# Hybrid decoder trunk on one core: router and shared gate of the first token tile placed ahead of the second tile's turns

## The reference, cut to what matters

```
x = layer_norm(ALPHA * x + g1 * mixed)
h = x * (1 + sc2) + sh2
scores = sigmoid(h @ w_router)            # 64 experts
# top 4 of 8 groups, then top 8 experts of a token, by scores + bias
ffn = (silu(h @ w_sh_gate) * (h @ w_sh_up)) @ w_sh_down + routed_moe(h, ...)
x = layer_norm(ALPHA * x + g2 * ffn)
```

## Time and profile before

| what | value |
|---|---|
| median of three timed runs | 1310.39 us |
| the three runs | 1309.18 to 1311.11 us |
| span of the profiled execution | 1307.3 us |
| PE busy | 1232.3 us (94%) |
| DVE busy | 492.9 us (38%) |
| ACT busy | 249.9 us (19%) |
| HBM read | 492.60 MB, 378 GB/s over the span |

### The profile page before, as it was taken

How to read it: one execution, slowest core, us unless ns; L and a number is a source line. 1 busy time by engine, 2 the same in 40 slices (tenths; PEclk the granted TensorE clock), 3 DMA queues, 4 the chain that set the end, 5 groups by cost and what they waited for, 6 DMA issues and landing times.

```text
span 1307.3 us, 28115 instructions
## 1 busy us (share of the span) xinstructions
PE 1232.3 (94%) x9342; PEld 771.9 (59%) x9342; DVE 492.9 (38%) x1111; ACT 249.9 (19%) x518; POOL 160.7 (12%) x587
## 2 busy tenths in 40 slices
PE   6999999999799999999988999999979999999995
PEld 3474566666466665566546557666646665566563
DVE  5666843222232222233347445222322322133335
ACT  1222211111111111111223312111111111111113
POOL 1000022111011111111000001111111111011110
PEclk9999999999899999999989999999999999899998
DMA  9999979999999999999867956999999999989992
GB/s 316 392 410 399 405 292 421 420 421 421 421 421 420 421 422 420 391 394 406 345 258 288 361 214 234 421 377 422 421 421 420 421 421 421 421 364 392 394 408 104
DMA packets 83921, 494.87 MB, mean 379 GB/s; under 512 B 11970, under 2 KB 20194, under 8 KB 29058
## 3 DMA queue, kind: packets, MB, share of 16 engines
q1 hardware_dynamic: 83842, 493.71, 92.7%
HBM read 492.60 MB, written 1.08 MB: 378 GB/s over the span
## 4 chain that ended last, share of the span: by engine, by line
PE 88%; DVE 4%; DMA 3%; issue 3%; SPq 2%; ACT 1%; DVEq 0%; ACTq 0%
PE ps L1028 32%; PE ps L1050 16%; PE ps L959 9%; PE ps L1071 8%; PE ps L969 5%; PE ps L688 3%; PE ps L881 3%; PE ps L909 2%; DMA w<-in_w_ada 2%; SPq L502 1%; PE ps L810 1%; PE ps L1000 1%; PE ps L1043 1%; PE ps L975 1%; DMA ring<-in_w_ada 1%
## 5 line engine op out<-in xcount | busy, mean ns | idle before, releaser
L1028 PE MATMUL ps<-ring,w 128*64 128x256 f32 (+1 forms) x3648 | 413.3, 385 | 0.5
L1028 PEld LDWEIGHTS ps<-ring,w 128*64 128x64 f32 (+1 forms) x3648 | 259.0, 127 | 68.6 <-issue 14.2
L1050 PE MATMUL ps<-ring,w 128*64 128x512 f32 (+1 forms) x912 | 207.7, 597 | 0.0
L1028 PE MATMUL ps<-flex,w 128*32 128x256 f32 x736 | 170.3, 391 | 26.5 <-issue 26.4
L1028 PE MATMUL ps<-w 128*32 128x256 f32 x736 | 170.8, 392 | 0.0
L1683 DVE SCALAR_TENSOR_TENSOR w<-ps,w 128x256 f32<-128x256 f32 x57 | 27.6, 484 | 374.1 <-PE ps L1028 374.1
L959 PE MATMUL ps<-hx,scat 128*128 128x512 f32 x472 | 138.3, 417 | 0.7 <-issue 0.7
L1669 DVE CAST scat<-ps 128x512 fp32r<-128x512 f32 x114 | 78.9, 692 | 158.9 <-PE ps L1050 158.9
L1028 PEld LDWEIGHTS ps<-flex,w 128*32 128x32 f32 x736 | 81.3, 113 | 84.7 <-issue 42.4
L1208 ACT ACTIVATE w<-ps 128x512 f32<-128x512 f32 x118 | 70.6, 598 | 290.4 <-PE ps L959 290.4
L1071 PE MATMUL ps<-scat 128*128 128x512 f32 x456 | 119.2, 403 | 0.0
(11 more groups left out here) (260 smaller groups left out, 1262.9 us busy)
## 6 DMA issues: line engine op xcount, KB each, us to landing
ring<-in_w_exp_gate SPq DMA_DIRECT2D x88, 1024.0 KB, 19.2
ring<-in_w_exp_up SPq DMA_DIRECT2D x88, 1024.0 KB, 22.3
ring<-in_w_exp_down SPq DMA_DIRECT2D x88, 1024.0 KB, 22.0
ring<-in_w_ada SPq DMA_DIRECT2D x30, 1024.0 KB, 10.9
w<-in_w_exp_gate SPq DMA_DIRECT2D x20, 1024.0 KB, 17.4
w<-in_w_exp_up SPq DMA_DIRECT2D x20, 1024.0 KB, 19.5
flex<-in_w_exp_gate SPq DMA_DIRECT2D x20, 1024.0 KB, 14.5
flex<-in_w_exp_up SPq DMA_DIRECT2D x20, 1024.0 KB, 16.1
```

Of the source, the lines that this page charges most:

```text
L1028: last = mm(ps[unit * g:unit * g + unit, bank, 0:F], hTb[:, kt, unit * g:unit * g + unit], weights(k)[:, kt, :], start=kt == 0, stop=kt == ...
L1050: last = mm(ps[unit * g:unit * g + unit, bank, :], midT[:, f, unit * g:unit * g + unit], down_w(k)[:, f, half * 512:(half + 1) * 512], sta ...
```

## The change

The fillers ahead of tile 1's turns go. In their place PE computes tile 0's logits and both halves of tile 0's shared gate, which need only what ACT has put out. After the turns, tile 1's logits and gate are computed by themselves, block by block as DVE delivers them, so each gate matmul has 128 moving columns instead of 256, and there are 32 of them instead of 16. The logits of both tiles now lie side by side in bank 1; tile 0's gate lies in bank 1 behind them and tile 1's in bank 3. The wait on esc_ready ahead of the up-projection goes, since bank 2 no longer holds logits. In layer 0 a wait on shsil_ready is added ahead of L945, which writes into bank 1. ACT's Exp reads its scores from one bank, and its Silu is two instructions, one for each tile.

```diff
--- before.py
+++ after.py
@@ -359,6 +359,7 @@
         JOB_BANK = (2, 3, 4, 5, 7)
         B_F, B_T, B_0, B_1 = 4, 5, 6, 7
         P0_COL = 448
+        GATE_BANK, GATE_COL = (1, 3), (NT * E, 0)
 
 
         names = """consts_in x_in c_in pos_in eps_set cT_done c32_ready bias_in mod_val_ready acc0_zeroed acc0_bias_in mod1_summed
@@ -901,28 +902,39 @@
                     for g in range(4):
                         last = mm(ps[32 * g:32 * g + 32, 0, :], ones[:, 0:32], acc0[:, g * 512:(g + 1) * 512], start=True, stop=True)
                     last.then_inc(s["p0_summed"], 1)
-                keep_busy(1, 6 if l == 0 else 4)
-                turn_normed(1)
-
                 def shared(w, bank, f, kts=range(KT)):
                     for kt in kts:
                         last = mm(ps[:, bank, f * T:(f + 1) * T], w[:, kt, f * P:(f + 1) * P], xT3[:, kt, :],
                                   start=kt == 0, stop=kt == KT - 1)
                     return last
 
+                def logits(j, kt):
+                    return mm(ps[:, 1, j * E:(j + 1) * E], xT3[:, kt, j * P:(j + 1) * P], router3[:, kt, :],
+                              start=kt == 0, stop=kt == KT - 1)
+
+                def shared_gate(j, f, kt):
+                    at_col = GATE_COL[j] + f * P
+                    return mm(ps[:, GATE_BANK[j], at_col:at_col + P], gate_w(3)[:, kt, f * P:(f + 1) * P],
+                              xT3[:, kt, j * P:(j + 1) * P], start=kt == 0, stop=kt == KT - 1)
+
                 pe.wait_ge(s["h2A_ready"], (l + 1) * KT)
                 pe.wait_ge(s["router_in"], (l + 1) * 16)
+                for kt in range(KT):
+                    logits(0, kt)
                 pe.wait_ge(s["sh_landed"], (l + 1) * 48)
+                for f in range(FT):
+                    for kt in range(KT):
+                        shared_gate(0, f, kt)
+                turn_normed(1)
                 for kt in range(KT):
                     pe.wait_ge(s["h2D_ready"], l * KT + kt + 1)
-                    for j in range(NT):
-                        last = mm(ps[:, 1 + j, 0:E], xT3[:, kt, j * P:(j + 1) * P], router3[:, kt, :],
-                                  start=kt == 0, stop=kt == KT - 1)
+                    last = logits(1, kt)
                     if kt == KT - 1:
                         last.then_inc(s["logits_done"], 1)
-                    shared(gate_w(3), 3, 0, (kt,))
-                shared(gate_w(3), 3, 1).then_inc(s["sh_gate_done"], 1)
-                pe.wait_ge(s["esc_ready"], l + 1)
+                    shared_gate(1, 0, kt)
+                for kt in range(KT):
+                    last = shared_gate(1, 1, kt)
+                last.then_inc(s["sh_gate_done"], 1)
                 shared(up_w(3), 2, 0)
                 for j in range(NT):
                     for half in range(2):
@@ -941,6 +953,7 @@
                     last = mm(ps[0:E, 0, 3 * E:3 * E + 1], sel[:, j, :], ones[:, 0:1], start=j == 0, stop=j == 1)
                 last.then_inc(s["rank_done"], 1)
                 if l == 0:
+                    pe.wait_ge(s["shsil_ready"], 1)
                     for i in range(4):
                         last = mm(ps[:, 1, P0_COL + i:P0_COL + 2 * KT:4], acc0[:, i * P:(i + 1) * P], one_of_4, start=True, stop=True)
                     last.then_inc(s["p0_columns"], 1)
@@ -1192,10 +1205,13 @@
                 table_for(ACT.Exp)
                 act.wait_ge(s["x1_ready"], l + 1)
                 act.wait_ge(s["logits_done"], l + 1)
-                fn(score, ps[:, 1:3, 0:E], ACT.Exp, scale=-1.0).then_inc(s["esc_ready"], 1)
+                fn(score, ps[:, 1, 0:NT * E].rearrange("p (j e) -> p j e", j=NT), ACT.Exp, scale=-1.0).then_inc(s["esc_ready"], 1)
                 table_for(ACT.Silu)
                 act.wait_ge(s["sh_gate_done"], l + 1)
-                fn(shsil, ps[:, 3, :], ACT.Silu).then_inc(s["shsil_ready"], 1)
+                for j in range(NT):
+                    last = fn(shsil.rearrange("p (f t) -> p f t", f=FT)[:, :, j * P:(j + 1) * P],
+                              ps[:, GATE_BANK[j], GATE_COL[j]:GATE_COL[j] + FT * P].rearrange("p (f n) -> p f n", f=FT), ACT.Silu)
+                last.then_inc(s["shsil_ready"], 1)
                 for n in range(4):
                     j, half = divmod(n, 2)
                     act.wait_ge(s["back_done"], l * 4 + n + 1)
```

## The result

The changed kernel takes 1316.62 us (median of four runs, 1314.40 to 1317.37) against 1309.81 for the kernel before on the same chip; the ratio is 1.0043 with a 95% interval of 1.0030 to 1.0055, so 5.6 us **slower**, with 3.9 to 7.2 as the interval. This ratio, here and in the experiments, is estimated from all runs of both kernels and need not equal that of the two medians (1.0052 here). The profiled execution took 1314.40 us with a span of 1312.6, 5.3 over the span of before.

A forecast was written before the change was run, and what follows sets the result against it. It took the expert rounds as paced by PE and the weight stream, which restarts on the order. Ranks 1.1 us earlier plus 5.2 us of clock fall gave +4.1 on 1310.39, so 1314.5 us, range 1311.0 to 1317.0.

The forecast's parts named there:

- The path: Both layers: only earlier rank, order and weight-stream restart shorten a layer; selection hangs on DVE, 15.63 us from turns in layer 0.
- The work ahead of the turns: Before tile 1's turns: 24 logits and gate calls at 0.2225 us, 5.34 us, replace fillers; turns +0.08 and +1.21 us.
- 0.38 for each call: Rival before the turns: weight loads not hidden under 128-column matmuls, 9.1 us for 24 calls, 3.8 us worse per layer; chance 0.03.
- The new wait: Before the rank: PE idles 4.1 us in layer 0 and 4.0 in layer 1; rank 1.04 and 0.08 us earlier.
- The clock: From rank to order: PE's clock falls to half level after the wait, costing 3.05 and 2.14 us, sum 5.2; chance 0.66.
- rival (a): Behind the rank's wait: clock falls but recovers as after weight waits, 1.70 us per layer, +2.3, 1312.7 us; chance 0.17.
- wholly at half level: Small matmuls from the rank to the up calls run entirely at half clock, costing 2.18 and 1.27 us.
- half of the four dense up calls: Up calls behind the small matmuls: half of them run at half clock, costing 0.87 us per layer.
- rival (b): Wait before the rank: clock does not fall, 1.04 + 0.08 us won, 1309.3 us; chance 0.11 together with one fall only.
- The sum: Whole kernel: -1.1 us from earlier ranks plus 5.2 us from the clock gives +4.1 us, 1314.5 us.

The follow-up runs named there:

- the first run with fillers: Changed kernel plus four filler matmuls before the wait for the selection, in both layers; 1311.79 us, ratio 1.0007 to the kernel before.
- the one with the columns late: Changed kernel with the four matmuls of four columns (layer 0) moved behind the order, idle kept; 1313.90 us, ratio 1.0027 to the kernel before.
- fillers in layer 0 alone: Changed kernel plus four filler matmuls before the wait for the selection, in layer 0 only; 1313.01 us, ratio 1.0016 to the kernel before.
- the shortened kernel: Kernel before with 12 shared-expert matmul calls left out in layer 1 alone, nothing reordered; 1310.76 us, ratio 1.0002 to the kernel before.
- turns first: Changed kernel rearranged: only tile 0's logits and first gate half before tile 1's turns, four up calls before the rank; 1308.25 us, ratio 0.9975 to kernel before.
- fillers, columns late: Changed kernel with four fillers before the selection wait in both layers and four-column matmuls behind the order; 1309.69 us, ratio 0.9993 to the kernel before.
- the last: Rearranged kernel with up calls split 2, 4, 2, four-column matmuls behind the order, plus one filler before the rank; 1306.63 us, ratio 0.9955 to kernel before.
- turns first, dense: Rearranged kernel with second up half split 2, 4, 2 around rank and order, four-column matmuls behind the order; 1308.06 us, ratio 0.9982 to kernel before.

## Why the prediction was right, point by point

*The path.* It named rank, order and the stream's restart as what decides, and the selection as tied to DVE. Both hold: the Exp was released by L1545, from the turns' start to the end of the selection it took 168.20 - 152.56 = 15.64 us (15.63 kept by the prediction), and the 3.78 us of the order came back to the hundredth at the end of a wait for weights 350 us later.

*The work ahead of the turns.* 5.34 us forecast; 152.56 - 147.10 = 5.46 in layer 0 and 784.16 - 778.81 = 5.35 in layer 1. Tile 0's 16 gate calls, 148.93 to 152.56, start every 0.227 us, and their weight loads run all through the same time, as the row of PEld shows:

```profile
148.88 3.65 PEld L917 LDWEIGHTS ps<-flex,ring 128*128 128x128 f32 x32
```

So the loads do run under the matmul ahead. The rule of the Trainium skill (TensorE: Matmul & The Clock Gate, What overlaps and what doesn't), by which the prediction worked out 0.38 for each call, does not hold here.

*The new wait.* Idle of 4.1 and 4.0 us forecast, 3.91 and 3.73 measured. From turns to rank 167.79 - 150.98 = 16.81 before and 168.26 - 152.56 = 15.70 after: 1.11 won; in layer 1 16.91 and 15.53, 1.38 won, of which the later turns give back 784.16 - 778.59 - (778.81 - 774.46) = 1.22. The forecast of 1.04 and 0.08 net (with turns 0.08 and 1.21 later) is met.

*The clock.* That it would fall in both layers (0.83 by the chances of the forecast and of rival (a)) is what the changed kernel shows in both layers, and with fillers in the wait the price is gone, but for the fall in layer 0 of the first run with fillers. The price was bounded at 1.70 to 4.5 a layer and put at 3.05 and 2.14; it measured 7.81 - 4.50 = 3.31 and 6.54 - 3.78 = 2.76, **6.1 in place of 5.2**. The sum came near partly by luck, because two of its errors offset each other. The price can be split at the start of the up calls and at their end, where the order's first matmul starts (L963 in the changed kernel, L950 before). In the kernel before it is at:

```profile
171.87 0.27 PE L950 MATMUL ps<-flex 64*1 64x64 f32 x2
798.86 0.27 PE L950 MATMUL ps<-flex 64*1 64x64 f32 x2
```

The small matmuls, let run "wholly at half level" for 2.18 and 1.27, cost 3.99 - 2.18 = 1.81 and (801.90 - 799.69) - 1.27 = 0.94: 0.7 us less together than forecast. The up calls, of which the prediction let half run at half level for 0.87 a layer, cost 3.40 - 1.90 = 1.50 and (805.61 - 801.90) - (798.86 - 796.77) = 1.62: 1.4 us more. So the step that was short is "half of the four dense up calls": nearly all of them ran at half. Rival (a) took the nearest row, a fall before dense work, and would have been 2.7 us short. Why the clock came back later here than in that row was argued from the small matmuls and is not shown: without the near-empty ones the stretch was at 0.50 all the same.

*A row misread.* The prediction takes the 1.00 of 130 to 137 as the clock after the wait of 2.17 us, but that wait ends at 136.77, so nearly all of the stretch lies ahead of its end. The work and the stretch behind it are these, and they do show 1.00:

```profile
137.77 7.03 PE L881 MATMUL ps<-w,flex 128*128 128x512 f32 x16
136.77:145.72 8.95, 8.95 (x32) 4.01 (x32) 8.65 (x6) 3.00 (x9) 0.00 (x0) 1.00 0.99 407
```

What rival (b) built on it fails all the same: that after a wait near 2.2 us the clock would stay. At this place, where all ten kernels have the same instructions, it stayed in some profiles and fell in others, as the last section shows.

*The sum.* Own loss of the stage: 3.31 - 1.11 + 0.20 (turns: 1.58 later, less the 1.38 by which PE came to 147.10 late) = 2.40 in layer 0, 2.76 - 1.38 + 1.22 = 2.60 in layer 1, 5.0 against the 4.1 forecast and 5.6 (3.9 to 7.2) measured. The measured median, 1316.62, lies 2.1 us over the forecast of 1314.5, near the upper end of its range. What PE was late by at 147.10 is not the change's: the clock had fallen after the wait ahead of tile 0's turns, as the first stretch of the changed kernel above shows (0.80 in 137.44 to 146.10), a place that both kernels share; so some 1.4 of the 5.3 us between the two profiled spans are not the change's. Why the median of the four runs lies 2.2 us above the profiled one was not seen; one run of four was profiled.

## What to carry to other kernels

Work taken off an engine that then waits for another engine's chain is worth only the lateness that the engine had (here 1.1 and 1.4 us), and if TensorE's clock falls in the wait, the work behind it on the path is what pays, small and dense matmuls alike (2.75 and 3.12 us of the 6.1 here). Before moving work ahead of a wait, add up the engine's new arrival against the wait's end, and fill what is left, with dense work or failing that with fillers: 1.1 us of idle was left in one version here and the clock still fell. A filler that looks idle can be holding the clock: look at the granted clock of the stretch behind it before taking it out.

## What the runs showed of the hardware that was not expected

The clock does not answer to one wait alone. With 3.5 to 3.9 us of idle ahead of the rank it fell every time, six of six: both layers of the changed kernel and of the one with the columns late, layer 1 with fillers in layer 0 alone, layer 1 of the shortened kernel (0.50 to 0.56 from rank to order). With about 2 us it went by the run. The wait ahead of tile 0's turns in layer 0 comes before anything that the ten kernels do differently, and five of their ten profiles have a fall behind it: after 1.91 us (changed), 2.23 (less work), 2.73 (turns first), 2.15 (fillers, columns late) and 2.19 (the last). The other five have none: after 2.17 (before), 2.15 (fillers), 0.86 (fillers in layer 0), 2.19 (turns first, dense) and 2.45 (columns late). So the length of the wait does not separate them. The same eight matmuls after the same 2.15 us, first with fillers alone, then with fillers and the columns late:

```profile
136.24 1.16 PE L891 MATMUL ps<-const,flex 128*128 128x128 f32 x8 [2.15 <-DVE flex L1542]
136.76 1.97 PE L891 MATMUL ps<-const,flex 128*128 128x128 f32 x8 [2.15 <-DVE flex L1542]
```

With 0.47 us ahead of the rank the clock was 0.73 from rank to order in one profile and 1.00 in another, for the same instructions; with 1.06 us it was 0.68 in layer 1 and with 1.25 us 1.00 in layer 0 of one execution. What made the difference was not found. The eight calls of `mix(1, 1)` behind those turns took 8.73 us in the changed kernel, with such a fall, and 7.03 in the kernel before, without it. So a gain of a microsecond in a stage like this one needs more than a few runs to be seen.
